# Turning C before B, and loading the first block's tables ahead of its weights, in a state-space hybrid block

## The reference, cut to what matters

```python
h_x = _rmsnorm(x, g_pre[l]) * (1 + sc_x) + sh_x
parts_x = _split_proj(h_x @ w_in[l])
u_c = h_c @ w_in[l][:, U_OFF:U_OFF + W_SSM]          # context, state-space input only
for d in range(2):                                   # two directions
    a_re, a_im, bb_re, bb_im = _zoh(lam_re, lam_im, log_dt, b_re, b_im)
    cr, ci = _scan_states(u_c_g, ..., None, rev)
    xr, xi = _scan_states(u_x_g, ..., h0, rev)
    ys_x.append(_readout(xr, xi, c_re, c_im))        # y = x_re C_re - x_im C_im
...
m = g0 * ya + g1 * yb + g2 * yc
return s + gate * _rmsnorm(m @ w_out, g_post)
```

## Time and profile before

| | us |
|---|---|
| median of 3 runs | 2051.77 |
| lowest and highest | 2050.26, 2053.57 |
| the profiled execution | 2049.25 |
| its span | 2047.5 |
| TensorE busy in the span | 1995.4 (97%) |
| VectorE busy | 1095.7 (54%) |
| ScalarE busy | 568.7 (28%) |

### The profile page before, as it was taken

How to read it: one execution, slowest core, us unless ns; L and a number is a source line. 1 busy time by engine, 2 the same in 40 slices (tenths; PEclk the granted TensorE clock), 3 DMA queues, 4 the chain that set the end, 5 groups by cost and what they waited for, 6 DMA issues and landing times.

```text
span 2047.5 us, 26609 instructions
## 1 busy us (share of the span) xinstructions
PE 1995.4 (97%) x9958; PEld 1628.1 (80%) x9958; DVE 1095.7 (54%) x1647; ACT 568.7 (28%) x795; POOL 32.3 (2%) x16
## 2 busy tenths in 40 slices
PE   4999999999999999999999999999999999999998
PEld 1568788888888888888888888888888888888886
DVE  4547699999998655544334343432433333333325
ACT  5324233333333322222222222222322222222222
POOL 0003200000000000000000000000000000000000
PEclk9999999999999999999999999999999999999999
DMA  9965666656663644443334444443233333334423
GB/s 362 363 203 167 172 152 151 150 147 146 153 152 110 188 128 127 134 138 107 95 94 145 126 132 137 129 132 113 62 97 98 93 103 92 95 100 155 174 99 128
DMA packets 392719, 289.08 MB, mean 141 GB/s; under 512 B 25268, under 2 KB 354460, under 8 KB 390804
## 3 DMA queue, kind: packets, MB, share of 16 engines
q1 hardware_dynamic: 382368, 283.96, 46.4%
q10 hardware_dynamic: 10292, 4.33, 1.4%
HBM read 268.59 MB, written 19.66 MB: 141 GB/s over the span
## 4 chain that ended last, share of the span: by engine, by line
PE 86%; DVE 1%; issue 0%; ACT 0%; DVEq 0%
PE ac L799 25%; PE ac L803 25%; PE ac L800 25%; PE ac L982 1%; PE ac L981 1%; PE ac L980 1%; PE ss L857 1%; PE ss L982 1%; PE ss L981 1%; PE ss L980 1%; DVE Og L1969 0%; PE ss L843 0%; PE ss L880 0%; PE ss L869 0%; PE ss L921 0%; PE ss L884 0%
## 5 line engine op out<-in xcount | busy, mean ns | idle before, releaser
L1609 DVE TENSOR_TENSOR wlo<-wslot,whi 128x1024 fp32r<-128x1024 f32 x309 | 378.4, 1225 | 642.8 <-ACT whi L1016 638.6
L1016 ACT ACTIVATE whi<-wslot 128x1024 fp32r<-128x1024 f32 x327 | 346.9, 1061 | 1264.0 <-PE ac L803 1052.7
L799 PE MATMUL ac<-hxh,whi 128*128 128x512 f32 x1664 | 652.8, 392 | 4.9 <-ACT whi L1016 4.9
L800 PE MATMUL ac<-hxl,whi 128*128 128x512 f32 x1664 | 648.8, 390 | 0.0
L803 PE MATMUL ac<-hxh,wlo 128*128 128x512 f32 x1664 | 411.1, 389 | 1.5 <-DVE wlo L1609 1.5
L799 PEld LDWEIGHTS ac<-hxh,whi 128*128 128x128 f32 x1664 | 313.2, 188 | 73.3 <-ACT whi L1016 5.3
L803 PEld LDWEIGHTS ac<-hxh,wlo 128*128 128x128 f32 x1664 | 312.4, 188 | 66.6 <-DVE wlo L1609 1.9
L800 PEld LDWEIGHTS ac<-hxl,whi 128*128 128x128 f32 x1664 | 313.3, 188 | 63.9
L799 PE MATMUL ac<-bah,whi 128*128 128x512 f32 x384 | 149.5, 389 | 0.0
L800 PE MATMUL ac<-bal,whi 128*128 128x512 f32 x384 | 149.4, 389 | 0.0
L803 PE MATMUL ac<-bah,wlo 128*128 128x512 f32 x384 | 94.8, 389 | 0.0
(11 more groups left out here) (366 smaller groups left out, 2034.9 us busy)
## 6 DMA issues: line engine op xcount, KB each, us to landing
wslot<-w_in SPq DMA_DIRECT2D x224, 512.0 KB, 3.8
ring<-w_ada SPq DMA_DIRECT2D x64, 512.0 KB, 8.3
gwt<-w_ada SPq DMA_DIRECT2D x128, 128.0 KB, 2.4
wslot<-w_out SPq DMA_DIRECT2D x32, 512.0 KB, 3.6
Ah<-ah_dram SPq DMA_DIRECT2D x16, 512.0 KB
Bh<-bh_dram SPq DMA_DIRECT2D x16, 512.0 KB
wslot<-proj_a SPq DMA_DIRECT2D x16, 512.0 KB, 4.1
wslot<-proj_b SPq DMA_DIRECT2D x16, 512.0 KB, 4.0
```

The costliest lines, as they stand in the source:

```text
L799: mm(ac[:, bank, :], w, xh, start=(v == 0 and q == 0), stop=False)
L800: mm(ac[:, bank, :], w, xl, start=False, stop=False)
L1016: cp = lambda o, i, scale=1.0: nc.scalar.activation(o, i, ACT.Copy, scale=scale)
L1609: tt(wlo[:, s, :], wslot[:, s, :], whi[:, (U0[k] + j) % 2, :].bitcast(F32), ALU.subtract)\
```

## The change

C is turned behind unit 8 and copied around the copy of unit 11; B is turned behind unit 10. The two stores of turned tables change places on SP. Behind `tab_load`, SP now issues `Ah` and `Bh`, ahead of the load of unit 16; U and the turned B are loaded behind the load of unit 17.

```diff
@@ SP, second half of the state-space input
             sp.dma_start(tab_b[:, :, n * 144:(n + 1) * 144], A[...]).then_inc(tab_out, 16)
+        late_unit(5)
         sp.wait_ge(p0_cp, 2)
-        sp.dma_start(tab_b[:, :, 544:800], B1[...]).then_inc(tab_out, 16)
-        late_unit(5)
+        sp.dma_start(tab_b[:, :, 288:544], C1[...]).then_inc(tab_out, 16)
...
         sp.wait_ge(p0_cp, 3)
-        sp.dma_start(tab_b[:, :, 288:544], C1[...]).then_inc(tab_out, 16)
+        sp.dma_start(tab_b[:, :, 544:800], B1[...]).then_inc(tab_out, 16)
         sp.wait_ge(tab_out, 16 * TAB_STORES)
         tab_load(0)
-        tap_load(0)
-        sp.wait_ge(u_out[0], 16)
-        u_load(0)
+        state_tables(0, [(side, d) for side in range(2) for d in range(2)])
         u_store(4)
@@ SP, stage k == 1, first block
-                    if k == 1 and j == 0 and isinstance(i, int) and i == 0:
-                        state_tables(0, [(side, d) for side in range(2) for d in range(2)])
+                    if k == 1 and j == 1 and isinstance(i, int) and i == 0:
+                        sp.wait_ge(u_out[0], 16)
+                        u_load(0)
+                        tap_load(0)
@@ PE
         def p0_b():
             pe.wait_ge(bb_done, 1)
-            pe.wait_ge(p0_cp, 1)
-            pe.wait_ge(uc_free, 4)
+            pe.wait_ge(p0_cp, 2)
         def p0_c():
-            pe.wait_ge(p0_cp, 2)
+            pe.wait_ge(p0_cp, 1)
+            pe.wait_ge(uc_free, 4)
             pe.wait_ge(b_in, 64)
...
                     if i == 0 and v == 0:
-                        (p0_b, p0_c)[j]()
+                        (p0_c, p0_b)[j]()
@@ ACT
         def raw_b():
-            act.wait_ge(p0_ps, 2)
+            act.wait_ge(p0_ps, 3)
         def raw_c(hs):
-            act.wait_ge(p0_ps, 3)
+            act.wait_ge(p0_ps, 2)
...
             hi(0, i, 2 * j + 2)
             if n == 0:
+                raw_c(range(H // 2))
+            if n == 1:
                 raw_b()
-            if n == 1:
-                raw_c(range(H // 2))
             hi(0, i, 2 * j + 3)
-            if n == 1:
+            if n == 0:
                 raw_c(range(H // 2, H))
```

More of the change, by code:

```diff
@@ L503, in _ @@
                 .then_inc(tab_out, 16)
+        late_unit(5)
         sp.wait_ge(p0_cp, 2)
-        sp.dma_start(tab_b[:, :, 544:800], B1[:, :, :].rearrange("p (b c) h -> p b (c h)", c=16)).then_inc(tab_out, 16)
-        late_unit(5)
+        sp.dma_start(tab_b[:, :, 288:544], C1[:, :, :].rearrange("p (b c) h -> p b (c h)", c=16)).then_inc(tab_out, 16)
         sp.wait_ge(an_done, 1)
@@ L514, in _ @@
         sp.wait_ge(p0_cp, 3)
-        sp.dma_start(tab_b[:, :, 288:544], C1[:, :, :].rearrange("p (b c) h -> p b (c h)", c=16)).then_inc(tab_out, 16)
+        sp.dma_start(tab_b[:, :, 544:800], B1[:, :, :].rearrange("p (b c) h -> p b (c h)", c=16)).then_inc(tab_out, 16)
         sp.wait_ge(tab_out, 16 * TAB_STORES)
         tab_load(0)
-        tap_load(0)
-        sp.wait_ge(u_out[0], 16)
-        u_load(0)
+        state_tables(0, [(side, d) for side in range(2) for d in range(2)])
         u_store(4)
```

## The result

The changed kernel's median is 2040.35 us (2037.59 to 2040.80, 4 runs), that of the kernel before in the same comparison 2051.02 (4 runs). The ratio is 0.9942 (95% interval 0.9926 to 0.9958), some 12 us less. Two later comparisons gave 0.9942 (0.9922 to 0.9962) and 0.9949 (0.9934 to 0.9964). The forecast was 2040.8 and 11.0 us less.

What follows compares the result with a forecast made beforehand. TensorE, busy 1995.4 of 2047.5 us, bounds the kernel, so only its idle time counts: -2.45 - 9.0 + 0.4 = -11.0 us, for a forecast median of 2040.8; range 2037.5 to 2048.

Steps and rivals of the forecast that it cites:

- The first wait (-2.45): TensorE's wait for finished B ahead of its transposes goes, since C is turned there instead: 2.45 us less.
- The stretch at units 17 and 18 (-9.0, clock included): TensorE's waits for `whi` of unit 17 and `wlo` of unit 18 go, with the lower clock: 9.0 us less.
- The end of the stores (207.0): B's store, issued about 198.7, is done at 207.0 (bounds 203.5 and 209); VectorE and tables start 5.8 us earlier.
- Unit 16 behind the tables (230, +0.4): Unit 16's load, now behind the tables, lands at 230; its high and low parts together cost TensorE 0.4 us.
- Half of the engines: Table loads use 8 of 16 DMA engines, as the 0.51 share suggested; with 16, unit 16 lands some 8 us sooner.
- unit 16 late by 2 to 5 us: Rival: TensorE waits for unit 16, lower clock follows; at 3.5 us late only 5.4 us gained, 2046.4; chance 22%.
- The steady-state price of 6.2 us for each table: Rival: four tables ahead of unit 16 delay it to 239.5, eating the gain; about 2052, no change; chance 12%.
- The queue did hold SP: Rival: SP's queue holds back the next units, unit 18 lands near 252 and TensorE waits; 2057, slower; chance 7%.

Runs made afterwards that it cites:

- `e_loads`: The kernel before with only the loads reordered: Ah and Bh ahead of unit 16, U and turned B behind unit 17; median 2041.79, ratio 0.9958.
- `e_u_ahead`: The changed kernel with the loads of U and turned B (tap table) put back ahead of Ah and Bh; median 2046.06, ratio to before 0.9973.
- `e_swap`: The changed kernel with the old order of loads, so only C turned and stored first remains; median 2045.88, ratio to before 0.9971.
- `e_split`: The changed kernel with each of the four table loads cut into eight loads of 16 rows; single run 2038.36 us.
- `e_x16`: The changed kernel with two more 512 KB loads, from 128 consecutive weight rows, between the tables and unit 16; single run 2044.42 us.
- `e_x8same`: The changed kernel with two more 512 KB loads, 8 rows each sent to 16, between the tables and unit 16; single run 2044.56 us.

## Why the prediction was right, and where it was off

The forecast was 2040.8 with 11.0 us less; the medians are 2040.35 and 10.5 to 12 less by the three ratios, the stretch itself 11.5. Point by point:

- **The first wait (-2.45)**: right, and by the mechanism named. `e_loads`, which keeps B first, still has 2.3 us, and nothing in the changed kernel took its place; the slack behind C's copies was 0.7 us against 0.8 forecast.
- **The stretch at units 17 and 18 (-9.0, clock included)**: right in size. `e_loads` shows it alone: 9.1. That the lower clock belongs to the price of such a wait shows in `e_u_ahead`: 6.4 us of wait cost 8.4, with the clock at 0.50 behind it.
- **The end of the stores (207.0)**: 207.8 in the profile whose unit 8 ends at 168.9, as in the working; B's store landed in 8.3 us there and in 8.1 in the first profile, against 8.3. But what was hung on it was wrong. The prediction let tables and VectorE start 5.8 us earlier and had unit 16 in time by 0.3 us only because of that. `e_loads` has the stores at 212.8 and unit 16 still in time, by 0.7 us. The earlier stores are needed only with the old order of loads (`e_swap`).
- **Unit 16 behind the tables (230, +0.4)**: the mis-sized term. The working carried over 23.8 us from the first table to the unit behind the tables and took off 1 to 2 for the bytes ahead. Measured are 18.0 to 19.4. The list of what had stood ahead was not whole: the tap table and the eight loads of U, 1024 pieces of 384 bytes, had been in front of the tables in the kernel before, and so had a second store of u; the working has only unit 16 and one store. The prediction said that U costs nothing while unit 18 is out in time, which is true where U stands now, and never priced what it had cost where it stood. `e_u_ahead` gives the price: 8.5 to 9.9 us for unit 16, and 8.4 in TensorE's stretch. Counted from the first table, as the working counts, it is 22.9 with U ahead. Not all of the 23.8 is explained so: `e_swap`, with the old order of loads, took 20.6 from its first table (219.81) to the copy of the unit behind them (240.38), and why the kernel before took 3 us more stays open. The slack of unit 16 was 2.1, 4.1 and 3.1 us in the three profiles where the working had 0.3, and the 0.4 were 0.
- **Half of the engines**: not borne out, as above. The 0.51 that the prediction took as agreement is no proof: `e_split` has 0.53 with the tables in the other form, though bound by their issue. It did not enter the sum.
- **The rivals**: unit 16 late by 2 to 5 us did not happen, but `e_u_ahead` shows what it looks like: a wait of 6.4 with the clock at 0.50 behind it. The steady-state price of 6.2 us for each table (28.6 us from the first table to the unit) is refuted by the changed kernel, with 18.0 to 19.4, and by `e_loads`, with 18.9. Its 239.5 also starts from 210.9, which the working doesn't derive; from its own first table at 207.35 it would have been 236.0. The queue did hold SP for 9.51 us, at a store behind unit 16, and unit 17's load was issued only at 226.07. That rival had its mechanism but not its price: unit 17 is wanted 5.4 us behind unit 16, and its copy was due at 234.4 at the earliest.
- **Ahead of the change**: that unit 8 ends at a time that differs by up to 5 us from one execution to the next was not in the prediction. In this profile it was 3.0 us later, and the stretch gained 0.5 more than forecast: so the span is 2.5 above what the sum gave for it, 2036.5. In the three profiles of the changed kernel it is all of the difference: their spans less the end of unit 8 are 1866.8, 1866.8 and 1866.7. That the median came within 0.5 us of the forecast is luck in part, since the runs lie between 2036.8 and 2042.4 for a reason that the sum doesn't hold.

## What to carry to other kernels

Where a wait hangs on the last transfer of a queue, list everything that was issued ahead of it in the last 10 to 20 us and ask of each when it is wanted: here the thing to move was the one wanted last (U, first read at 256, 22 us behind unit 16). Moving it together with the tables was worth 9.1 us, earlier stores with the old order of loads 4.8 (7.3 less the first wait); moving U alone gave 4 in the median, so neither piece alone gets it all. Don't price such a piece by its bytes: 0.5 MB of U and tap table cost 8.5 to 9.9 us where 1 MB in larger pieces cost 6. Whether the nine issues or the small pieces make it dear, no run here separates. Two cures of one lateness don't add up, so try each alone; and read a change of a few us from the stretch that it touches, not from the span of one execution.

## What the runs showed of the hardware

- Eight loads of 48 KB in pieces of 384 bytes, with one of 128 KB, delayed a weight unit behind them by 8.5 to 9.9 us (`e_u_ahead`, 28.3 us against 18.4 to 19.8); 1 MB in two loads with pieces of 4 KB delayed it by about 6 (24.8 to 25.3 against 18.0 to 19.4).
- The issue of a store of u (384 KB in 128 pieces) on SP's queue took 0.46 us in front of unit 16 in the changed kernel, and 9.51 right behind it, with four table loads and the unit issued in the 5 us ahead. The same store took 12.33 us in `e_u_ahead` and 12.77 in `e_x16`, where more stood in front.
- After 6.4, 3.6 and 2.6 us of idle time TensorE ran at a granted 0.50 (1.2 GHz) for some us and the stretch lost 2.0, 1.7 and 1.8 us beyond the wait; after 2.8 us in `e_x16` the window shows 1.00 and the loss beyond the wait is 0.3. After the 3.0 of `e_swap`, too, the window from 254 to 258 shows 1.00, and after the 2.45 of the kernel before nothing was lost. So the length of the gap alone does not tell whether the clock falls: it fell behind 2.6 us and stayed behind 3.0. The first window below is `e_x8same`, the second `e_x16`, both with a wait for unit 16's `whi` just before:

```profile
238.00:240.00 2.00, 2.00 (x7) 1.52 (x6) 2.00 (x1) 1.86 (x3) 1.95 (x2) 0.50 0.88 234
```

```profile
238.00:240.00 2.00, 2.00 (x9) 1.65 (x10) 1.97 (x2) 0.62 (x1) 2.00 (x1) 1.00 0.70 160
```
